# Block products of a conv-FFN kept in two PSUM chains, down tiles between them on three bank pairs, weight rounding on ScalarE

## The reference

```python
def conv_ffn(h, w_up, conv_w, conv_b, w_down):
    u = h @ w_up                                   # 1024 -> 2 x 2816
    u = lax.conv_general_dilated(u, ...) + conv_b  # causal, width 3, each channel by itself
    gate, val = jnp.split(u, 2, axis=-1)
    return (jax.nn.silu(gate) * val) @ w_down      # 2816 -> 1024
```

## Time and profile before

| | us |
|---|---|
| median of 3 runs (2634.44 to 2636.25) | 2634.8 |
| span of the profiled execution | 2631.1 |
| PE busy | 2439.2 (93%) |
| DVE busy | 1926.0 (73%) |
| POOL busy | 1462.1 (56%) |
| ACT busy | 846.4 (32%) |

### The profile page before, as it was taken

How to read it: one execution, slowest core, us unless ns; L and a number is a source line. 1 busy time by engine, 2 the same in 40 slices (tenths; PEclk the granted TensorE clock), 3 DMA queues, 4 the chain that set the end, 5 groups by cost and what they waited for, 6 DMA issues and landing times.

```text
span 2631.1 us, 31515 instructions
## 1 busy us (share of the span) xinstructions
PE 2439.2 (93%) x11916; PEld 1957.4 (74%) x11916; DVE 1926.0 (73%) x2195; ACT 846.4 (32%) x1439; POOL 1462.1 (56%) x1123
## 2 busy tenths in 40 slices
PE   7899999989999999996899999978989999999993
PEld 5688887777777777773677787757777777777772
DVE  3676673796888888789666777662796788888878
ACT  3344451451111111114346465652441111111112
POOL 2222114547888888884441323114546888888883
PEclk9999999999999999998999999978999999999997
DMA  4122134401111111122121212043311111111112
GB/s 153 56 65 73 60 134 152 147 30 57 49 49 48 57 49 61 52 88 102 53 65 39 87 52 80 18 160 120 128 57 51 54 49 48 49 57 48 57 63 104
DMA packets 51236, 191.97 MB, mean 73 GB/s; under 512 B 5904, under 2 KB 6416, under 8 KB 47376
## 3 DMA queue, kind: packets, MB, share of 16 engines
q1 hardware_dynamic: 39184, 148.92, 17.1%
q10 hardware_dynamic: 11904, 41.05, 4.1%
HBM read 146.43 MB, written 29.36 MB: 67 GB/s over the span
## 4 chain that ended last, share of the span: by engine, by line
PE 73%; DVE 16%; ACT 4%; issue 3%; DMA 2%; SPq 1%; ACTq 0%; POOL 0%; POOLq 0%; DVEq 0%
PE ps L1208 9%; PE ps L1209 9%; PE ps L1210 9%; PE ps L1230 6%; PE ps L1231 6%; PE ps L1232 6%; PE ps L1039 3%; PE ps L1011 2%; PE ps L1013 2%; PE ps L1012 2%; PE ps L1076 2%; PE ps L1056 2%; PE ps L1131 1%; PE ps L996 1%; PE ps L1133 1%
## 5 line engine op out<-in xcount | busy, mean ns | idle before, releaser
L2079 DVE TENSOR_TENSOR a<-a,ps 128x1024 f32<-128x1024 f32 x336 | 409.4, 1220 | 196.7 <-PE ps L1232 188.5
L748 POOL CAST w_hi<-w_raw 128x1024 fp32r<-128x1024 f32 x78 | 84.9, 1088 | 801.8 <-PE ps L1013 274.8
L1230 PE MATMUL ps<-hid,ring 128*128 128x512 f32 x704 | 294.7, 419 | 30.0 <-DVE a L2079 16.7
L1575 ACT ACTIVATE cy<-cx,cv 128x1024 f32<-128x1024 f32 x76 | 94.8, 1247 | 675.4 <-DVE cx L2050 675.4
L830 POOL TENSOR_TENSOR ring<-w_raw,ring 128x512 fp32r<-128x512 f32 x206 | 298.6, 1449 | 16.5
L1231 PE MATMUL ps<-hid,ring 128*128 128x512 f32 x704 | 278.1, 395 | 0.0
L1232 PE MATMUL ps<-hid,ring 128*128 128x512 f32 x704 | 277.0, 393 | 0.0
L828 POOL CAST ring<-w_raw 128x512 fp32r<-128x512 f32 x206 | 167.9, 815 | 184.2 <-PE ps L1232 92.8
L1209 PE MATMUL ps<-h,ring 128*128 128x512 f32 x608 | 237.2, 390 | 0.0
L1208 PE MATMUL ps<-h,ring 128*128 128x512 f32 x608 | 237.1, 390 | 0.0
L1210 PE MATMUL ps<-h,ring 128*128 128x512 f32 x608 | 236.8, 389 | 0.0
(11 more groups left out here) (274 smaller groups left out, 6504.1 us busy)
## 6 DMA issues: line engine op xcount, KB each, us to landing
w_raw<-in_W SPq DMA_DIRECT2D x166, 512.0 KB, 3.2
raw_d<-in_W SPq DMA_DIRECT2D x44, 512.0 KB, 3.2
h<-o_dram ACTq DMA_DIRECT2D x2, 6144.0 KB, 21.2
x_dram<-x ACTq DMA_DIRECT2D x6, 2048.0 KB, 7.3
x<-x_dram SPq DMA_DIRECT2D x2, 4096.0 KB, 13.3
dsw<-draw SPq DMA_DIRECT2D x64, 128.0 KB, 2.3
o_dram<-most SPq DMA_DIRECT2D x6, 1024.0 KB, 4.9
o_dram<-dost SPq DMA_DIRECT2D x6, 1024.0 KB, 4.5
```

The costliest lines, as they stand in the source:

```text
L1230: pe.matmul(out, wh, xh, start=True, stop=False)
L2079: dve.tensor_tensor(a[:, f, :], a[:, f, :], src, ALU.add).then_inc(acc_done, 1)
```

## The change

**Two chains.** The products of a hidden tile go into two banks only. P1, P6, P7 and P4 follow each other in one (the chain keeps adding into it), P2 alone and then P5 and P3 in the other. Only P1, P2 and P5 clear the bank. So PE forms sums that DVE formed: ACT copies the bank after P1, P6, P5 and P4, and DVE adds after P2, P7 and P3: four copies and three additions in place of one copy and six additions. A product that goes on in a bank waits until the step before has been read. `cx` shrinks from four slots to two (one hidden tile in place of two).

**Down tiles.** They use banks 2 to 7 as three pairs, and tile f waits for the addition three tiles before. They are spread between the products: a pass is P1, d6 of n-2, P2, d7 of n-2, P6, P5, d0, d1, P7, d2, d3, P3, d4, P4, d5 (the latter six of n-1). `hid` holds one hidden tile (from n = 1 on), so the rounded part of tile n is written only after d7 of n-1.

**Weights.** From hidden tile 4 on ACT writes the rounded part of each item and POOL only the subtraction; POOL's sums come after the G1 and G2 items. SP loads G, D, V in that order.

Of the moved lines: 828 and 830 become ACT 1636 and POOL 853, 2050 becomes 2115, 2079 becomes 2144, 1284 becomes 1329, 1575 becomes 1620, 1579 becomes 1640, 1585 becomes 1646, 2065 becomes 2130, 2069 becomes 2134.

```diff
-PRODUCTS = ["P1", "P6", "P2", "P5", "P7", "P4", "P3"]
+PRODUCTS = ["P1", "P2", "P6", "P5", "P7", "P3", "P4"]
...
+CHAIN = {"P1": 0, "P6": 0, "P7": 0, "P4": 0, "P2": 1, "P5": 1, "P3": 1}
+OPENS = ["P1", "P2", "P5"]
+COPIED = ["P1", "P6", "P5", "P4"]
+ADDED = ["P2", "P7", "P3"]
...
+        old = [("dn", n - 2, f) for f in (range(KT) if n == PLAIN else range(6, KT))]
+        new = [("dn", n - 1, f) for f in range(KT)]
+        p1, p2, p6, p5, p7, p3, p4 = [("up", n, c) for c in PRODUCTS]
+        half = len(old) // 2
+        out += [p1] + old[:half] + [p2] + old[half:] + [p6, p5]
+        if n < HT - 1:
+            out += new[0:2] + [p7] + new[2:4] + [p3] + new[4:5] + [p4] + new[5:6]
         else:
-            out += ups[:-1] + tiles[:1] + ups[-1:] + tiles[1:]
+            out += new[0:2] + [p7] + new[2:3] + [p3] + new[3:4] + [p4] + new[4:]
...
+            out += [(n, "G1"), (1, "d1"), (n, "G2"), (1, "d2")]
         else:
-            out += [(n, c) for c in ("G1", "S2", "G2", "S1", "S3")]
-        if n == HT - 1:
-            out += [(n, "V2"), (n, "S4"), (n - 1, "d1"), (n - 1, "d2")]
-        else:
-            out += [(n, "V2"), (n - 1, "d1"), (n, "S4"), (n - 1, "d2")]
+            out += [(n, "G1"), (n, "G2")]
+        out += [(n, "S2"), (n, "S1"), (n - 1, "d1"), (n, "S3"), (n, "S4"), (n - 1, "d2"), (n, "V2")]
...
+BY_ACT = ITEMS[ITEMS.index((PLAIN + 1, "G1")):]
...
-        cx = at("cx", 42, 4)
+        cx = at("cx", 42, 2)
...
+            return bank((n - PLAIN + CHAIN[name]) % 2)
+        def down_bank(n, f):
+            return 4 + 2 * (f % 2) if n == 0 else 2 + 2 * ((KT * (n - 1) + f) % 3)
+        def hid_part(n, low):
+            return hid[:, (2 if n else 0) + low, :]
...
+                    if PLAIN < n < HT:
+                        sp.wait_ge(item_ready, item_count(layer, n - 1, "V2"))
+                        load_ffn(layer, n, "V")
...
+                    if (n, name) in BY_ACT:
+                        pool.wait_ge(item_cast, cast_count(layer, n, name))
+                        pool.tensor_tensor(lo, raw[name], hi.bitcast(F32), ALU.subtract).then_inc(item_ready, 1)
+                        return
...
+                def bank_free(n, name):
+                    if n == PLAIN and name in ("P1", "P2"):
+                        pe.wait_ge(conv_done, conv_count(layer, PLAIN - 1, 0))
                         return
-                    if place < 4:
-                        n, place = n - 1, place + len(PRODUCTS)
-                    before = PRODUCTS[place - 4]
-                    if before == "P1":
-                        pe.wait_ge(bank_copied, (HT - PLAIN) * layer + n - PLAIN + 1)
-                    else:
-                        pe.wait_ge(c_sum, result_count(layer, n, RESULT_OF[before]))
+                    before = {"P1": "P3", "P2": "P4", "P6": "P1", "P5": "P2", "P7": "P6", "P3": "P5", "P4": "P7"}[name]
+                    wait_read(pe, layer, n - 1 if name in ("P1", "P2") else n, before)
...
+                        pe.matmul(out, wh, xh, start=k == 0 and name in OPENS, stop=False, skip_group_check=True)
...
-                        pe.wait_ge(acc_done, acc_count(layer, n, f) - 2)
+                        pe.wait_ge(acc_done, acc_count(layer, n, f) - 3)
                     f4 = f % 4
                     wh, wl = at_[:, 0, f4 * P:(f4 + 1) * P], at_[:, 0, HB + f4 * P:HB + (f4 + 1) * P]
                     for half in range(2):
-                        out = bank(4 + 2 * (f % 2) + half)
-                        xh, xl = half_of(hid, 2 * (n % 2), half), half_of(hid, 2 * (n % 2) + 1, half)
+                        out = bank(down_bank(n, f) + half)
...
+            def bank_copy(layer, n, name):
+                v, half = {"P1": (0, 0), "P6": (0, 1), "P5": (1, 1), "P4": (1, 0)}[name]
+                act.wait_ge(up_done, up_count(layer, n, name))
+                if n == PLAIN:
+                    act.wait_ge(dn_done, down_count(layer, 0, KT - 1))
+                else:
+                    act.wait_ge(conv_done, conv_count(layer, n - 1, v))
+                act.activation(half_of(cx, v, half), up_bank(n, name), ACT.Copy).then_inc(bank_copied, 1)
...
+                def cast(n, name):
+                    if (n, name) not in BY_ACT:
+                        return
+                    sort, m_, what = FREE_AFTER[n, name]
+                    if sort == "up":
+                        act.wait_ge(up_done, up_count(layer, m_, what))
+                    else:
+                        act.wait_ge(dn_done, down_count(layer, m_, what))
+                    if name[0] == "S":
+                        act.wait_ge(w_sum, 4 * ((HT - PLAIN) * layer + n - PLAIN) + {"S1": 1, "S3": 2, "S2": 3, "S4": 4}[name])
+                    else:
+                        c = name[0].upper()
+                        act.wait_ge(f_loaded[c], 16 * (HT * layer + n + 1))
+                    act.activation(item_parts(n, name)[0], raw_item(name), ACT.Copy).then_inc(item_cast, 1)
...
+                    if n >= 2:
+                        act.wait_ge(dn_done, down_count(layer, n - 1, KT - 1))
+                    act.activation(hid_part(n, 0), cy[:, 0, :], ACT.Copy).then_inc(hid_hi, 1)
...
+                        gate(n - 1)
+                    bank_copy(layer, n, "P1")
+                    cast(n - 1, "d1")
+                    hid_top(n - 1)
+                    cast(n, "S3")
+                    cast(n, "S4")
+                    bank_copy(layer, n, "P6")
+                    cast(n - 1, "d2")
+                    bank_copy(layer, n, "P5")
+                    cast(n, "V2")
+                    cast(n + 1, "G1")
+                    cast(n + 1, "G2")
+                    act.wait_ge(bank_added, added_count(layer, n, "P3"))
                     act.wait_ge(hid_lo, u0 + n)
                     tap(n, 0)
-                gate_and_split(HT - 1)
+                    bank_copy(layer, n, "P4")
+                    act.wait_ge(bank_copied, copied_count(layer, n, "P4"))
+                    tap(n, 1)
+                    cast(n + 1, "S2")
+                    cast(n + 1, "S1")
+                cast(HT - 1, "d1")
+                gate(HT - 1)
+                cast(HT - 1, "d2")
+                hid_top(HT - 1)
...
+                def bank_add(n, name):
+                    v, half, copied = {"P2": (0, 0, "P1"), "P7": (1, 1, "P5"), "P3": (0, 1, "P6")}[name]
+                    dst = half_of(cx, v, half)
+                    dve.wait_ge(up_done, up_count(layer, n, name))
+                    dve.wait_ge(bank_copied, copied_count(layer, n, copied))
+                    dve.tensor_tensor(dst, dst, up_bank(n, name), ALU.add).then_inc(bank_added, 1)
...
+                        add(n - 2, 6)
+                    bank_add(n, "P2")
+                    for f in range(4 if n == PLAIN else 7, KT):
+                        add(n - 2, f)
                     hid_tail(n - 1)
-                    for name in ("W", "C22", "U3"):
-                        result(n, name)
-                    result(n, "C21")
+                    add(n - 1, 0)
+                    add(n - 1, 1)
+                    bank_add(n, "P7")
+                    add(n - 1, 2)
                     if n < HT - 1:
-                        for f in range(KT):
-                            add(n - 1, f)
-                    result(n, "C12")
-                add(HT - 2, 0)
+                        add(n - 1, 3)
+                    bank_add(n, "P3")
+                    if n < HT - 1:
+                        add(n - 1, 4)
+                        conv_tile(n, 0)
+                        add(n - 1, 5)
+                    else:
+                        add(n - 1, 3)
+                        conv_tile(n, 0)
                 conv_tile(HT - 1, 1)
-                add(HT - 2, 1)
-                add(HT - 2, 2)
-                conv_tile(HT - 1, 0)
-                add(HT - 2, 3)
                 product(HT - 1)
                 add(HT - 2, 4)
-                add(HT - 2, 5)
                 hid_tail(HT - 1)
-                for f in range(6, KT):
+                for f in range(5, KT):
```

More of the change, by code:

```diff
@@ L539, in up_count, with copied_count, added_count, wait_read @@
             return len(UPS) * layer + UPS.index((n, name)) + 1
[L541 to L545 removed]
+        def copied_count(layer, n, name):
+            return len(COPIED) * ((HT - PLAIN) * layer + n - PLAIN) + COPIED.index(name) + 1
+        def added_count(layer, n, name):
+            return len(ADDED) * ((HT - PLAIN) * layer + n - PLAIN) + ADDED.index(name) + 1
+        def wait_read(eng, layer, n, name):
+            if name in COPIED:
+                eng.wait_ge(bank_copied, copied_count(layer, n, name))
+            else:
+                eng.wait_ge(bank_added, added_count(layer, n, name))
+        def up_bank(n, name):
+            return bank((n - PLAIN + CHAIN[name]) % 2)
[3 more added lines that the diff above has]
+            return hid[:, (2 if n else 0) + low, :]
+        def raw_item(name):
```

(29 more changed lines are left out.)

89 lines of the change are left out of this document (26 added, 63 removed).

## The result

| | before | changed |
|---|---|---|
| median of the runs, us | 2635.5 | 2600.0 |
| profiled span, us | 2631.1 | 2596.9 |
| PE busy, us | 2439.2 (93%) | 2408.7 (93%) |
| DVE busy | 1926.0 (73%) | 1823.5 (70%) |
| POOL busy | 1462.1 (56%) | 1207.4 (46%) |

The ratio of the runs is 0.9868, with a 95% interval of 0.9854 to 0.9882: faster, as forecast, by some 35 us where 28 were forecast. 2600.0 lies on the very edge of the range, 2600 to 2621. The profiled spans differ by 34.2.

A forecast was written before the change was run, and what follows sets the result against it. PE's matmul pace was taken as the bound, with later down tiles waiting for DVE's additions. Per layer 13.1 + 2.7, less 1.7 at the end, nets 14.1; two layers take 28.2 off 2634.8, giving 2607, range 2600 to 2621.

The forecast's parts named there:

- Steady passes: Seventeen passes, n = 4 to 20: each falls from 30.72 to 29.95 us, 13.1 us a layer gained.
- the spare times: Within a pass: P6's copy ends 1.7 us before P7 wants the bank, the lower part 1.2 before d0.
- three bank pairs, and down tiles between products: In each pass, at most two tiles in a row, each waiting for the third addition before: PE has 29.95 us.
- Pass of n = 3: From first product of n = 3 to P1 of n = 4: no PE wait left, 2.7 us a layer gained.
- the 2604 from that first product on: From the first product of n = 3 on, the matmuls stay the same 2604; the forecast's counting starts there.
- The end: After the last passes of a layer: one hidden buffer makes DVE idle and PE wait, losing 1.7 us a layer.
- The two waits before d7 and d0 of n = 21: At a layer's end PE waits 3 to 4 us each before tile 7 of n = 20 and tile 0 of n = 21.
- I take 6.5: Layer end, n = 21: copy, tap, two convolution steps, multiplication and hand-overs after P4 take 6.0 to 7.0 us, taken as 6.5.
- The idle "2.7": Layer end: DVE idles from addition 4 through one tile (1.36), one ACT operation (1.06) and hand-overs, 2.7 us.
- The late hidden tile: Rival, chance 0.13: POOL delays DVE's chain in every pass, d0 starts 0.3 to 0.4 us late; 2619.
- ACT's queue: Rival, chance 0.09: slow casts and POOL operations make P6's copy 1.7 us late for P7 in each pass; 2665.
- the pace: Rival, chance 0.10: down tiles' slower matmul steps come from DVE reading banks, so 0.5 of 0.77 us stays; 2625 at most.

The follow-up runs named there:

- the turned closing order: Changed kernel with DVE's addition 4 of n = 20 ahead of tile 21's second convolution, addition 5 between multiplication and hidden tile's lower part: 2590.6 us.
- two small edits: Changed kernel with POOL's n = 3 sums put back ahead of item G1: 2612.1 us; kernel before with those sums waiting for T3's rests: 2621.0 us.
- the run with late sums: Kernel before with one wait more, POOL making the sums of n = 3 only after DVE has written the rests of T3: 2621.0 us.

## Why the prediction was right, and where not

**Steady passes: right.** 0.80 us a pass where 0.77 was forecast; the pace is 0.2267 rather than 0.2269. No wait was left before P7, P5, d0 or a later tile, and the spare times came within 0.2. Before d0 that is in part luck: beside POOL the value half's convolution steps took 2.39 and 2.20 where the walk had 1.83 and 1.51, so the multiplication ended 8.2 us into the pass and not 7.5, and the lower part made it good with 1.44 in place of 1.80. And the step's heading, "three bank pairs, and down tiles between products", joined two causes, and the runs part them: in the chains, spread tiles on two pairs give 29.92, three pairs in a row remove the waits for additions, and of the two only the spread lets the chains run at pace. What the third pair is worth, on the turned closing order, is 13 us, at the ends and in the pass of n = 3.

**Pass of n = 3: right**, 2.7 a layer.

**The start: the step that failed.** The sum began at "the 2604 from that first product on", and the stretch ahead of it stood in no sentence. The re-ordered items were on the table: the sums stand behind G1 and G2 and, for n = 3, behind two down items. I walked this through the steady pass only. I also had the mechanism in hand (a multiplication of 2.36 beside POOL, 1.23 without) but asked of it only where it would hurt. The moved sums freed DVE's chain, the chain freed ACT's first sums, PE's wait fell by 4.8 us and its clock stayed up: 6.9 and 6.4 a layer, shown from both sides by two small edits.

**The end: right in kind, mis-sized.** The two waits before d7 and d0 of n = 21 came (4.77 and 3.69, forecast 3 to 4), and DVE idled. "I take 6.5" from P4 to the end of the multiplication was 7.8: POOL's subtractions of the two down items, which ACT's late roundings released just then, stretched a convolution step to 2.19 and the multiplication to 2.10, where the step had assumed 1.3 and 1.23 without POOL. The idle "2.7" was 4.17, since d7 ran at the lower clock, its matmuls 0.43 apart. 1.3 + 1.5, less 0.6 by which P4 came sooner after the first product, is the 2.2 us by which the first layer's end lost more than forecast. In the second layer the same terms (7.8, and 3.95 of idle time) give 2.0 of its 3.3; where the rest went I have not traced.

**The rivals.** The late hidden tile, ACT's queue and the pace did not come: in the passes ACT's casts took 0.61 to 0.63 on average and its copies 0.59, as the row of 0.62 had them. ACT was the wrong place to fear and also no help: without its roundings the passes are the same. The late hidden tile rested on the stretching of DVE beside POOL, and that came: the two steps of 2.39 and 2.20 above; only the lateness did not. The Trainium skill (SBUF — State Buffer, "Who interferes with whom") also says that a DVE instruction with at most one input in SBUF, outside the two-port modes, does not contend with GpSimd. The trace agrees: on the page of the changed kernel the additions from PSUM into the accumulator take 1.216 us on average, beside POOL's work or not (none of the 336 over 1.23), while DVE's multiplication goes from 1.21 to 2.31. The same convolution step that took 2.20 took 1.28 where one input is a bank, beside a POOL subtraction:

```profile
L2144 DVE TENSOR_TENSOR a<-a,ps 128x1024 f32<-128x1024 f32 x336 | 408.4, 1216 | 178.4 <-PE ps L1272 166.4
...
577.46 1.28 DVE L2124 SCALAR_TENSOR_TENSOR cy<-ps,cv,cy 128x1022 f32<-128x1022 f32 x1
...
576.79 1.30 POOL L870 TENSOR_TENSOR ring<-raw_d,ring 128x512 fp32r<-128x512 f32 x1
```

So POOL did not stretch the additions wherever they stood in the pass; the convolutions from `cx`, the multiplication and the lower part it did. A stretched step here lost 0.9 to 1.1 us, somewhat less than the 1.29 of a POOL subtraction by itself.

**The sum.** The start adds 13.3 us to the forecast gain, the passes 1.0, the ends take 5.4 away: 28.2 + 8.9 = 37.1, the FFNs' measured gain. The forecast was right in its main term; that the total came this near, and on the edge of the range and not beyond it, is luck: two misses of opposite sign met.

## What to carry to other kernels

When a change re-orders an engine's queue, walk the new order through the start and the end of the loop as well as through a steady pass: of 37 us gained here, 13 came from three POOL operations that moved 20 us later, before the loop that the change was about. Where two engines stretch each other, the question to ask is what else lies in that time, and one added wait may answer it on the old kernel already. And part a change before keeping it: one of its parts (ACT's roundings) was worth nothing in the passes and cost at the end, and the third pair told only in the pass of n = 3 and at the ends. What was not parted here is the spread from the chains.

## What the runs showed that I had not expected

- Four sums on DVE took 5.52 us beside POOL's work and 2.48 with POOL idle, 0.76 us more for each. POOL is held up too: the first sum, which starts beside DVE's rests in the run with late sums, took 3.48 against 1.29 in the passes.
- More work on POOL can mean less delay. With the roundings on POOL, POOL was busy 468 us of the seventeen passes in place of 333, yet DVE for 365 in place of 378. When ACT hands POOL its subtractions, they start together with DVE's convolutions; that this alignment is the cause is only inferred.
- A PE wait of 6.4 us cost 2 us more after it, with nine matmuls 0.43 us apart; behind one of 1.6 us they were 0.23 apart and the granted clock was 1.00.
- Executions differ by up to 3.3 us before the first FFN and by 4.5 between the two, in code that the edits leave alone; a stretch of the timeline that the edit touches tells a few microseconds apart where the total does not.
